# Who adds the last rows: two of four final adds move from VectorE to ScalarE and Pool

## The chip, the cores and the metric

The kernel runs on one core of one Trainium2 chip. The metric is the device time of one execution in microseconds (us), as the median of several executions. One profiled execution stands beside them; its span runs from the first to the last instruction of the core.

## The reference

One inference step of a two-layer encoder, for 256 rows of a new stream (the prompt) and 32 rows of a running one (the decode rows). Each layer is attention and then a feed-forward part; the second layer's is a mixture of 8 experts, of which every row uses two. Only the very end matters here: the weighted sum over the experts, added to the residual.

```python
def moe(h, router, wg, wu, wd):
    ...
    out = jnp.zeros_like(h)
    for e in range(N_EXPERTS):
        out = out + comb[..., e:e + 1].astype(h.dtype) * swiglu(h, wg[e], wu[e], wd[e])
    return out
...
        xp = xp + channel_mix(rms_norm(xp, ln_ffn[l]), l, *fw)      # (1, 256, 1024)
...
        xs = xs + channel_mix(rms_norm(xs, ln_ffn[l]), l, *fw)      # (1, 32, 1024)
```

`xp` and `xs` after the second layer are the outputs `y_prompt` and `y_sample`.

## The kernel before

Each engine has a program of its own, written out by hand in one order, and they meet at semaphores. The 288 rows are three tiles: two of 128 prompt rows and one of 32 decode rows. The residual of all three is `xres` (128 partitions x 3 tiles x 1024 columns) in SBUF; the decode rows are partitions 0 to 31 of tile 2. `ps` is the PSUM, eight banks of 512 float32 columns.

The experts run one after another. TensorE multiplies the gathered rows of one expert with weights that SP streams in. All experts but the last add their rows to a table in DRAM (`sum_rows`), by an indirect DMA of Pool. While the last expert runs, Pool loads that table back into `xres` (L893, L894; semaphore `sums_in`) and makes the 0/1 matrices `sel` (L898) that put each row of the last expert's result in its place.

The end of the program, after the last expert's products, works in two halves of 512 columns:

- ScalarE scales the result out of PSUM into `y_hi` (L1258 for half 0, L1264 and L1266 for the two parts of half 1; L1262 puts the last quarter of the columns in `y_out` first). VectorE takes the remainder of the split into `y_lo` (L1822, three times; semaphore `y_low`).
- TensorE multiplies `sel` with `y_hi` (L2448) and with `y_lo` (L2451), for three tiles each. Half 0 goes to the banks 0, 1 (prompt) and 4 (decode), half 1 to the banks 2, 3 and 5. When the second tile of a half is finished, and again when the third is, it raises `rows_full`.
- VectorE adds the banks to `xres` (L1829 both prompt tiles, L1831 the decode rows) and raises `rows_summed` after each.
- SP waits for those and issues four transfers to the outputs (L747 `y_p`, L750 `y_s`), 512 KB and 64 KB a half, then waits until all four have landed.

```python
banks = (2 * half, 2 * half + 1, 4 + half)
```

Of the kernel before, what the change touches and what calls it, by code (L numbers as in the profile page):

```python
# [22 lines left out]
ALU = mybir.AluOpType  # L23
ACT = mybir.ActivationFunctionType
# [5 lines left out]
SEQ, DEC = 256, 32  # L30
# [188 lines left out]
def build(nc, a, out, consts):  # L219
# [35 lines left out]
    with ExitStack() as ctx:  # L255
        def sb(name, shape, dt=F32):
            return ctx.enter_context(nc.sbuf_tensor(name, shape, dt))

        def sem(name):
            return ctx.enter_context(nc.semaphore(name))  # L260
# [8 lines left out]
        xres = sb("xres", [P, 3, D])  # L269
# [115 lines left out]
        y_out = carve("y_out", D)  # L385
# [21 lines left out]
        ps = ctx.enter_context(nc.psum_tensor("ps", [P, 8, 512], F32))  # L407
# [104 lines left out]
        sums_in = sem("sums_in")  # L512
# [3 lines left out]
        y_low = sem("y_low")  # L516
        rows_full = sem("rows_full")
        rows_summed = sem("rows_summed")
        result_out = sem("result_out")

        xs_rows = nc.dram_tensor("xs_rows", (SPARE, D), F32, kind="Internal").ap()
# [3 lines left out]
        def C(name, rows=P):  # L525
            at, w = CONST[name]
            return cst[0:rows, at:at + w]
# [14 lines left out]
        def pair(key, rows=P):  # L542

            *_, b, n = found(key)
            return ps[0:rows, b:b + n, :].rearrange("p a b -> p (a b)")
# [11 lines left out]
        def wide(b, rows=P):  # L557

            return ps[0:rows, b:b + 2, :].rearrange("p a b -> p (a b)")
# [6 lines left out]
        def wait_full(eng, key):  # L566
            filled, _, i, n, *_ = found(key)
            eng.wait_ge(filled[i], n)

        def wait_out(eng, key):  # L570
            _, emptied, i, n, *_ = found(key)
            eng.wait_ge(emptied[i], n)
# [75 lines left out]
        def _(sp):  # L648
# [36 lines left out]
            for key in plan:  # L685
# [8 lines left out]
                if key[0] == "wo":  # L694
                    _, _, c, typ = key
# [47 lines left out]

            for half in range(2):
                c0 = 512 * half
                sp.wait_ge(rows_summed, 2 * half + 1)
                sp.dma_start(out["y_p"][0].rearrange("(t p) d -> p t d", p=P)[:, :, c0:c0 + 512], xres[:, 0:2, c0:c0 + 512])\  # L747
                    .then_inc(result_out, 16)
                sp.wait_ge(rows_summed, 2 * half + 2)
                sp.dma_start(out["y_s"][0][:, c0:c0 + 512], xres[0:DEC, 2, c0:c0 + 512]).then_inc(result_out, 16)  # L750
            sp.wait_ge(result_out, 64)

# [1 line left out]
        def _(pool):  # L754
# [6 lines left out]
            for l in range(DEPTH):  # L761
                for n, name in enumerate(("b_qn_norm", "b_kn_norm")):
                    c = DEPTH * (n + 1) + l
# [132 lines left out]
            pool.wait_ge(row_split, 1)  # L896
            for t in range(3):
                pool.tensor_scalar(sel[0:SLOTS, t, :], C("iota", SLOTS), float(P * t), row_at[0:SLOTS, 0:1], ALU.add, ALU.is_equal).then_inc(sel_ready, 1)  # L898
            pool.wait_ge(stored, 16 * (DEPTH * 10))


        @block.scalar
        def _(act):
            A = nc.scalar.activation
# [45 lines left out]
            for l in range(DEPTH):  # L950
                for step in ACT_ORDER[l]:
# [20 lines left out]
                    elif kind == "zev":  # L972

                        t, c = which
# [243 lines left out]
            def expert(j, final):  # L1218

                A(warm[:, 0:1], warm[:, 0:1], ACT.Silu)  # L1220

                def silu(c):

                    w = WIDTH[c] // 2
                    act.wait_ge(unit_used, j * len(EXPERT) + (unit["gate", c, 3] + 1))
                    if c:
                        act.wait_ge(act_done, j * CHUNKS + c)
                    A(sgm[0:HALF, BANK:BANK + w], ps[HALF:P, 1, 0:w], ACT.Copy).then_inc(gate_part, 1)  # L1228
                    A(sgm[:, 0:w], ps[:, 0, 0:w], ACT.Silu)
                    act.wait_ge(gate_sum, j * CHUNKS + (c + 1))  # L1230
                    A(sgm[0:HALF, BANK:BANK + w], sgm[0:HALF, BANK:BANK + w], ACT.Silu).then_inc(silu_done, 1)

                def up_half(c):

                    w = WIDTH[c] // 2
                    act.wait_ge(unit_used, j * len(EXPERT) + (unit["up", c, 3] + 1))
                    if c:
                        act.wait_ge(am_ready, j * CHUNKS + c)
                    A(act_m[0:HALF, BANK:BANK + w], ps[HALF:P, 3, 0:w], ACT.Copy).then_inc(up_part, 1)  # L1239

                def output():

                    act.wait_ge(row_moved, j + 1)
                    act.wait_ge(unit_used, j * len(EXPERT) + len(EXPERT))
                    A(sgm[0:HALF, BANK:2 * BANK], ps[HALF:P, 7, :], ACT.Copy).then_inc(y_tail, 1)
                    for s_ in range(4):
                        g, h = s_ // 2, s_ % 2
                        A(y_out[GRAN * g:GRAN * g + GRAN, BANK * h:BANK * h + BANK], ps[GRAN * s_:GRAN * s_ + GRAN, 6, :], ACT.Copy)\
                            .then_inc(y_copied, 1)
                    act.wait_ge(y_copied, j * 4 + 4)  # L1250
                    act.wait_ge(y_sums, j + 1)
                    A(y_out[0:SLOTS, :], y_out[0:SLOTS, :], ACT.Copy, scale=slot_gate[0:SLOTS, 0:1]).then_inc(y_taken, 1)

                def last_output():

                    act.wait_ge(row_moved, j + 1)
                    act.wait_ge(y_half, 1)
                    A(y_hi[0:SLOTS, 0:512], ps[0:SLOTS, 6, :], ACT.Copy, scale=slot_gate[0:SLOTS, 0:1]).then_inc(y_high, 1)  # L1258
                    for g in range(MAIN):
                        if D_TAIL * (g + 1) > 512:  # L1260
                            act.wait_ge(y_half, 2)
                        ins = A(y_out[GRAN * g:GRAN * g + GRAN, D_LANE:D], wide(6)[SLOTS:P, D_TAIL * g:D_TAIL * g + D_TAIL], ACT.Copy)  # L1262
                    ins.then_inc(y_tail, 1)
                    A(y_hi[0:SLOTS, 512:D_LANE], ps[0:SLOTS, 7, 0:D_LANE - 512], ACT.Copy, scale=slot_gate[0:SLOTS, 0:1]).then_inc(y_high, 1)  # L1264
                    act.wait_ge(y_tail, j + 1)
                    A(y_hi[0:SLOTS, D_LANE:D], y_out[0:SLOTS, D_LANE:D], ACT.Copy, scale=slot_gate[0:SLOTS, 0:1]).then_inc(y_high, 1)  # L1266

                for c in range(CHUNKS):
                    silu(c)
                    up_half(c)  # L1270
                if final:
                    last_output()
                else:
                    output()

            last = act.snap(more * NE + (NE - 1))
            with act.Fori(0, last) as j:
                expert(j, False)
            expert(last, True)


        @block.vector
        def _(dve):
            V = nc.vector
# [128 lines left out]
            for l in range(DEPTH):  # L1413
                for step in DVE_ORDER[l]:
# [204 lines left out]
                    elif kind == "wd":  # L1619

                        t, c = which
# [203 lines left out]
            def result_rows(half):  # L1825

                c = slice(512 * half, 512 * half + 512)
                dve.wait_ge(rows_full, 2 * half + 1)
                V.tensor_tensor(xres[:, 0:2, c], xres[:, 0:2, c], ps[:, 2 * half:2 * half + 2, :], ALU.add).then_inc(rows_summed, 1)  # L1829
                dve.wait_ge(rows_full, 2 * half + 2)  # L1830
                V.tensor_tensor(xres[0:DEC, 2, c], xres[0:DEC, 2, c], ps[0:DEC, 4 + half, :], ALU.add).then_inc(rows_summed, 1)  # L1831

            result_low(1, ps[0:SLOTS, 6, :], slice(0, 512))
            result_low(2, ps[0:SLOTS, 7, 0:D_LANE - 512], slice(512, D_LANE))
            result_low(3, y_out[0:SLOTS, D_LANE:D], slice(D_LANE, D))
            dve.wait_ge(sums_in, 32)
            result_rows(0)
            result_rows(1)


# [679 lines left out]
```

## Time and profile before

| what | value |
|---|---|
| runs | 1217.24, 1217.74, 1217.84 us; median 1217.74 us |
| the profiled execution, its own time | 1219.62 us |
| its span | 1217.8 us |
| TensorE (matmul) busy | 1196.2 us, 98% of the span |
| VectorE busy | 552.8 us, 45% |
| ScalarE busy | 329.3 us, 27% |
| Pool busy | 79.0 us, 6% |
| DMA, mean over the span | 286 GB/s |

The profiled execution is one run with the profiler on: durations inside it are compared with each other, and its own time need not be that of the runs. Busy shares are means over a span with many stages, and say little of the last six microseconds. In rows of a timeline a number after "x" is how many instructions one row stands for; an instruction's duration can reach into that of the next on its engine.

### The profile page before, as it was taken

Reading aid. Unit: us, or ns where it says so; the run is one execution under the profiler, and the core shown is the slowest. Engines: PE = TensorE matmul, PEld = TensorE weight load, DVE = VectorE, ACT = ScalarE, POOL = GpSimd, SP = SyncE. Lnnn points to the kernel's source line nnn. Section 1 sums busy time; section 2 is a strip of 40 time slices with the busy share of each in tenths; the row PEclk is TensorE's granted clock in tenths of the full one; section 3 lists DMA queues with packets and bytes.
Section 4 is the critical chain, followed back from the end, with each engine's and each line's share of the span. In section 5 each row is a group of like instructions: output and inputs, shape, how many; then the busy total and the mean of one; then the engine's idle time right before and its main releaser. Section 6 shows DMA issues by size and latency. Waiting matters only on the chain.

```text
span 1217.8 us, 24127 instructions
## 1 busy us (share of the span) xinstructions
PE 1196.2 (98%) x10189; PEld 627.6 (52%) x10189; DVE 552.8 (45%) x1027; ACT 329.3 (27%) x602; POOL 79.0 (6%) x175
## 2 busy tenths in 40 slices
PE   8999999999999999999999999999999999999898
PEld 5466599999995466533333333333333333333255
DVE  1666644444414568533433434344264245334334
ACT  2557544333324565411210210200200201201101
POOL 4231000000001102000000000000000100100100
PEclk9999999999999999999999999999999999999999
DMA  9161195444250153699999999999999999999995
GB/s 302 31 165 61 42 304 173 150 163 154 88 173 31 24 117 107 242 410 399 410 388 411 402 395 413 398 400 414 399 402 414 399 399 415 389 411 414 393 410 233
DMA packets 113913, 348.51 MB, mean 286 GB/s; under 512 B 8401, under 2 KB 33841, under 8 KB 103617
## 3 DMA queue, kind: packets, MB, share of 16 engines
q1 hardware_dynamic: 108656, 335.55, 72.9%
q0 software_dynamic: 3648, 10.60, 3.1%
q10 hardware_dynamic: 1552, 1.56, 0.4%
q8 instruction: 41, 0.67, 0.2%
q14 instruction: 16, 0.12, 0.0%
HBM read 339.65 MB, written 8.04 MB: 286 GB/s over the span
## 4 chain that ended last, share of the span: by engine, by line
PE 90%; DMA 4%; DVE 3%; ACT 2%; SPq 0%; issue 0%; DVEq 0%; ACTq 0%
PE ps L2342 35%; PE ps L2349 17%; PE ps L2247 12%; PE ps L1991 8%; PE ps L2263 6%; DMA ring_more<-in_moe_w_gate 2%; DMA ring<-in_w_in 2%; PE ps L2064 1%; PE ps L2072 1%; PE ps L2328 1%; PE ps L2124 1%; PE ps L2139 1%; PE ps L2177 1%; PE ps L2187 1%; PE ps L2004 1%; PE ps L2333 1%
## 5 line engine op out<-in xcount | busy, mean ns | idle before, releaser
L2342 PE MATMUL ps<-ring,xg 128*32 128x512 f32 (+1 forms) x1792 | 203.9, 562 | 0.4 <-DVE xg L1723 0.4
L1774 DVE STREAM_TRANSPOSE am<-act_m 32x256 f32<-32x256 f32 (+1 forms) x288 | 172.5, 599 | 4.7
L2342 PE MATMUL ps<-ring_more,xg 128*32 128x512 f32 (+1 forms) x1280 | 144.6, 554 | 4.2 <-DMA ring_more<-in_moe_w_gate 4.2
L2342 PEld LDWEIGHTS ps<-ring,xg 128*32 128x32 f32 x1792 | 58.8, 110 | 119.7 <-issue 118.9
L1300 DVE TENSOR_TENSOR w_lo<-ring,w_hi 128x2048 fp32r<-128x2048 f32 (+1 forms) x34 | 75.8, 2230 | 96.1 <-ACT w_hi L914 96.1
L1991 PE MATMUL ps<-ring,hT 128*128 128x512 f32 x256 | 115.2, 596 | 0.1
L1759 DVE TENSOR_TENSOR act_m<-act_m,ps 64x512 f32<-64x512 f32 (+1 forms) x24 | 15.2, 635 | 213.3 <-ACT act_m L1239 213.3
L2349 PE MATMUL ps<-ring,xg 128*32 128x512 f32 (+1 forms) x896 | 110.0, 562 | 0.0
L2247 PE MATMUL ps<-hT_hi,w_hi 128*128 128x288 f32 x352 | 104.3, 296 | 0.5 <-DVE hT_lo L1642 0.5
L2247 PE MATMUL ps<-hT_lo,w_hi 128*128 128x288 f32 x352 | 103.8, 295 | 0.0
L2247 PE MATMUL ps<-hT_hi,w_lo 128*128 128x288 f32 x352 | 103.5, 294 | 0.0
L2342 PE MATMUL ps<-ring_more,am 128*32 128x512 f32 x784 | 95.7, 592 | 0.0
L1228 ACT ACTIVATE sgm<-ps 64x512 f32<-64x512 f32 (+1 forms) x24 | 13.4, 558 | 271.9 <-PE ps L2342 271.9
L914 ACT ACTIVATE w_hi<-ring 128x2048 fp32r<-128x2048 f32 (+1 forms) x34 | 63.3, 1863 | 82.4 <-PE ps L2247 44.1
L2342 PEld LDWEIGHTS ps<-ring_more,xg 128*32 128x32 f32 x1280 | 41.7, 111 | 84.5 <-issue 77.9
L1751 DVE TENSOR_TENSOR sgm<-sgm,ps 64x512 f32<-64x512 f32 (+1 forms) x24 | 15.2, 635 | 146.9 <-ACT sgm L1228 146.9
L2349 PE MATMUL ps<-ring_more,xg 128*32 128x512 f32 (+1 forms) x640 | 77.2, 553 | 0.0
L1991 PEld LDWEIGHTS ps<-ring,hT 128*128 128x128 f32 x256 | 46.8, 190 | 51.6 <-issue 51.4
L2247 PEld LDWEIGHTS ps<-hT_hi,w_hi 128*128 128x128 f32 x352 | 66.0, 187 | 0.9 <-DVE hT_lo L1642 0.9
L2247 PEld LDWEIGHTS ps<-hT_hi,w_lo 128*128 128x128 f32 x352 | 66.3, 188 | 0.0
L2247 PEld LDWEIGHTS ps<-hT_lo,w_hi 128*128 128x128 f32 x352 | 66.1, 188 | 0.0
L1239 ACT ACTIVATE act_m<-ps 64x512 f32<-64x512 f32 (+1 forms) x24 | 13.4, 558 | 182.4 <-PE ps L2342 182.4
(369 smaller groups left out, 1577.4 us busy)
## 6 DMA issues: line engine op xcount, KB each, us to landing
ring<-in_moe_w_up SPq DMA_DIRECT2D x48, 1024.0 KB, 18.6
ring_more<-in_moe_w_down SPq DMA_DIRECT2D x48, 1024.0 KB, 18.1
ring<-in_moe_w_gate SPq DMA_DIRECT2D x32, 1024.0 KB, 16.5
ring_more<-in_moe_w_gate SPq DMA_DIRECT2D x32, 1024.0 KB, 19.9
ring<-in_moe_w_down SPq DMA_DIRECT2D x32, 1024.0 KB, 16.2
ring_more<-in_moe_w_gate SPq DMA_DIRECT2D x32, 768.0 KB, 19.8
ring<-in_moe_w_up SPq DMA_DIRECT2D x32, 768.0 KB, 14.8
ring_more<-in_moe_w_up SPq DMA_DIRECT2D x16, 1024.0 KB, 17.4
```

The source lines that it names most:

```text
L914: A(hi[:, 0:size], src[:, 0:size], ACT.Copy).then_inc(hi_ready, 1)
L1228: A(sgm[0:HALF, BANK:BANK + w], ps[HALF:P, 1, 0:w], ACT.Copy).then_inc(gate_part, 1)
L1239: A(act_m[0:HALF, BANK:BANK + w], ps[HALF:P, 3, 0:w], ACT.Copy).then_inc(up_part, 1)
L1300: V.tensor_tensor(lo[:, 0:size], src[:, 0:size], hi[:, 0:size].bitcast(F32), ALU.subtract).then_inc(lo_ready, 1)
L1751: V.tensor_tensor(part, part, ps[0:HALF, 1, 0:w], ALU.add).then_inc(gate_sum, 1)
L1759: V.tensor_tensor(part, part, ps[0:HALF, 3, 0:w], ALU.add).then_inc(up_sum, 1)
L1774: ins = V.transpose(am[GRAN * q:GRAN * q + GRAN, c % 2, 0:nk, GRAN * g:GRAN * g + GRAN], src)
L1991: ins = mm_(pair(key), hT[:, k, TOFF[t]:TOFF[t] + P], slot(wk, 4, 512)[:, k % 4, :], start=(k == 0), stop=(k == KD - 1))
L2247: ins = mm_(pair(key)[:, 512 * f:512 * f + TOK], w[:, k, f * P:(f + 1) * P], x[:, k, :], start=(k == 0 and m == 0), stop=(k == KD - 1 and ...
L2263: ins = mm_(pair(("dn", i, d // 2))[:, 512 * (d % 2):512 * (d % 2) + TOK], w[:, k, d * P:(d + 1) * P], x[:, kk, :], start=(kk == 0 and m = ...
L2342: ins = mm_(ps[GRAN * s_:GRAN * s_ + GRAN, b, 0:half], x[:, GRAN * g:GRAN * g + GRAN], w[:, half * h:half * h + half], start=(n == 0), sto ...
L2349: ins = mm_(ps[r0:r0 + GRAN, b + 1, 0:half], x[:, GRAN * 2:SLOTS], w[:, half * h:half * h + half], start=(n < 2), stop=(n >= n_last - 1))
```

## The change

The decode rows of each half go another way. ScalarE, which has nothing left to do at that point, copies their PSUM bank into `y_out` in SBUF (new semaphore `decode_rows`). Pool, which can't read PSUM here, adds `y_out` to `xres` (new semaphore `decode_summed`). VectorE keeps the two prompt adds. `y_out` still holds the last quarter of the expert's columns for the third `y_lo` product, so ScalarE first waits for all three of these (`y_low` at 3). SP issues its four transfers in the same order, and waits for `decode_summed` ahead of each `y_s`.

```diff
@@ SP
-                sp.wait_ge(rows_summed, 2 * half + 1)
+                sp.wait_ge(rows_summed, half + 1)
                 sp.dma_start(out["y_p"][0]...
-                sp.wait_ge(rows_summed, 2 * half + 2)
+                sp.wait_ge(decode_summed, half + 1)
                 sp.dma_start(out["y_s"][0]...
@@ Pool, behind the three sel
+            pool.wait_ge(sums_in, 32)
+            for half in range(2):
+                c = slice(512 * half, 512 * half + 512)
+                pool.wait_ge(decode_rows, half + 1)
+                pool.tensor_tensor(xres[0:DEC, 2, c], xres[0:DEC, 2, c], y_out[0:DEC, c], ALU.add).then_inc(decode_summed, 1)
             pool.wait_ge(stored, 16 * (DEPTH * 10))
@@ ScalarE, behind the last expert
+            act.wait_ge(y_low, 3)
+            for half in range(2):
+                c = slice(512 * half, 512 * half + 512)
+                act.wait_ge(rows_full, 2 * half + 2)
+                A(y_out[0:DEC, c], ps[0:DEC, 4 + half, :], ACT.Copy).then_inc(decode_rows, 1)
@@ VectorE, result_rows(half)
                 V.tensor_tensor(xres[:, 0:2, c], xres[:, 0:2, c], ps[:, 2 * half:2 * half + 2, :], ALU.add).then_inc(rows_summed, 1)
-                dve.wait_ge(rows_full, 2 * half + 2)
-                V.tensor_tensor(xres[0:DEC, 2, c], xres[0:DEC, 2, c], ps[0:DEC, 4 + half, :], ALU.add).then_inc(rows_summed, 1)
```

How the instructions stand at the end of three engines' programs (the line numbers of the changed kernel are larger by 2 to 12). VectorE, from the three `y_lo` products to its last instruction, before:

```order
L1822 SCALAR_TENSOR_TENSOR y_lo<-ps,slot_gate,y_hi 96x512 [waits y_high]
L1822 SCALAR_TENSOR_TENSOR y_lo<-ps,slot_gate,y_hi 96x256 [waits y_high]
L1822 SCALAR_TENSOR_TENSOR y_lo<-y_out,slot_gate,y_hi 96x256 [waits y_high]
L1829 TENSOR_TENSOR xres<-xres,ps 128x2x512 [waits rows_full,sums_in]
L1831 TENSOR_TENSOR xres<-xres,ps 32x512 [waits rows_full]
L1829 TENSOR_TENSOR xres<-xres,ps 128x2x512 [waits rows_full]
L1831 TENSOR_TENSOR xres<-xres,ps 32x512 [waits rows_full]
```

and of the change:

```order
L1834 SCALAR_TENSOR_TENSOR y_lo<-ps,slot_gate,y_hi 96x512 [waits y_high]
L1834 SCALAR_TENSOR_TENSOR y_lo<-ps,slot_gate,y_hi 96x256 [waits y_high]
L1834 SCALAR_TENSOR_TENSOR y_lo<-y_out,slot_gate,y_hi 96x256 [waits y_high]
L1841 TENSOR_TENSOR xres<-xres,ps 128x2x512 [waits rows_full,sums_in]
L1841 TENSOR_TENSOR xres<-xres,ps 128x2x512 [waits rows_full]
```

The two adds of 32x512 are gone, and the second prompt add follows the first. ScalarE, its end in the changed kernel (before, its program ended with the fifth of these rows):

```order
L1265 ACTIVATE y_hi<-ps,slot_gate 96x512 [waits y_half,row_moved]
L1269 ACTIVATE y_out<-ps 32x256 x2
L1269 ACTIVATE y_out<-ps 32x256 [waits y_half]
L1271 ACTIVATE y_hi<-ps,slot_gate 96x256
L1273 ACTIVATE y_hi<-y_out,slot_gate 96x256 [waits y_tail]
L1291 ACTIVATE y_out<-ps 32x512 [waits rows_full,y_low]
L1291 ACTIVATE y_out<-ps 32x512 [waits rows_full]
```

Two copies out of PSUM stand behind everything that ScalarE did before. Pool, its end in the changed kernel (before, the last wait stood right behind the three `sel`):

```order
L897 CAST row_at<-slot_row 96x1
L900 TENSOR_SCALAR sel<-cst,row_at 96x128 [waits row_split]
L900 TENSOR_SCALAR sel<-cst,row_at 96x128 x2
L905 TENSOR_TENSOR xres<-xres,y_out 32x512 [waits decode_rows,sums_in]
L905 TENSOR_TENSOR xres<-xres,y_out 32x512 [waits decode_rows]
L255 UNCONDITIONAL_BRANCH [waits stored]
```

Two adds from SBUF to SBUF stand ahead of Pool's last wait. The order of TensorE's instructions and of SP's is the same in both kernels.

## Rows read from the trace of the kernel before

**Rows 1.** The page, chain that ended last: shares of the span by engine.

```profile
PE 90%; DMA 4%; DVE 3%; ACT 2%; SPq 0%; issue 0%; DVEq 0%; ACTq 0%
```

**Rows 2.** Timeline, 1205 to 1218: start us, us, engine, line, operation.

```profile
1210.27 0.86 PE L2451 MATMUL ps<-y_lo,sel 96*128 96x512 f32 x3
...
1210.88 0.48 DVE L1822 SCALAR_TENSOR_TENSOR y_lo<-y_out,slot_gate,y_hi 96x256 fp32r<-96x256 f32 x1
...
1211.27 1.21 DVE L1829 TENSOR_TENSOR xres<-xres,ps 128x1024 f32<-128x1024 f32 x1
...
1211.69 0.86 PE L2451 MATMUL ps<-y_lo,sel 96*128 96x512 f32 x3
1212.40 0.67 DVE L1831 TENSOR_TENSOR xres<-xres,ps 32x512 f32<-32x512 f32 x1
1212.51 0.42 SPq L747 DMA_DIRECT2D out_y_p<-xres  x1
1213.00 1.20 DVE L1829 TENSOR_TENSOR xres<-xres,ps 128x1024 f32<-128x1024 f32 x1
1213.10 0.36 SPq L750 DMA_DIRECT2D out_y_s<-xres  x1
1214.13 0.67 DVE L1831 TENSOR_TENSOR xres<-xres,ps 32x512 f32<-32x512 f32 x1
1214.23 0.39 SPq L747 DMA_DIRECT2D out_y_p<-xres  x1
1214.83 0.34 SPq L750 DMA_DIRECT2D out_y_s<-xres  x1
```

**Rows 3.** The chain that ended last, 1209 to 1218, its last piece.

```profile
1214.20 0.60 DVE xres L1831
```

**Rows 4.** SP queue's waits, 1170 to 1218: total us, times, longest.

```profile
SPq L255 <- DMA out_y_s<-xres: 2.2, 1, 2.2
```

**Rows 5.** DMA issues, 1205 to 1218: count, KB each, us to landing.

```profile
out_y_p<-xres SPq DMA_DIRECT2D x2, 512.0 KB, 2.9
out_y_s<-xres SPq DMA_DIRECT2D x2, 64.0 KB, 2.5
```

**Rows 6.** Windows of 0.1 us; the last three columns: TensorE clock, DMA share, GB/s.

```profile
1213.40:1213.50 0.10, 0.00 (x0) 0.00 (x0) 0.10 (x1) 0.00 (x0) 0.00 (x0) 1.00 0.50 184
...
1215.00:1215.10 0.10, 0.00 (x0) 0.00 (x0) 0.00 (x0) 0.00 (x0) 0.00 (x0) 1.00 0.47 144
1215.10:1215.20 0.10, 0.00 (x0) 0.00 (x0) 0.00 (x0) 0.00 (x0) 0.00 (x0) 0.64 0.54 185
1216.80:1216.90 0.10, 0.00 (x0) 0.00 (x0) 0.00 (x0) 0.00 (x0) 0.00 (x0) 0.50 0.28 82
```

**Rows 7.** Groups by line and shape, ScalarE: busy us, mean ns, idle before.

```profile
L1248 ACT ACTIVATE y_out<-ps 32x512 f32<-32x512 f32 x28 | 16.5, 589 | 0.7
```

**Rows 8.** Groups by line and shape, Pool: busy us, mean ns, idle before.

```profile
L898 POOL TENSOR_SCALAR sel<-cst,row_at 96x128 fp32r<-96x128 f32 x3 | 2.2, 726 | 0.1
...
L818 POOL COPY qkb<-kr 128x256 f32<-128x256 f32 x4 | 1.6, 402 | 19.4 <-PE ps L2088 19.4
...
L786 POOL TENSOR_TENSOR rc_a_q_norm<-cst,gains 128x128 f32<-128x128 f32 x2 | 0.9, 456 | 0.2
...
L787 POOL TENSOR_TENSOR rs_b_qr_norm<-cst,gains 128x32 f32<-128x32 f32 x2 | 0.5, 244 | 0.0
```

**Rows 9.** Timelines of ScalarE and of Pool near 1036.

```profile
1035.29 1.15 ACT L1252 ACTIVATE y_out<-y_out,slot_gate 96x1024 f32<-96x1024 f32 x1
...
1036.52 0.18 POOL L856 TENSOR_TENSOR tick<-cst 128x1 f32<-128x1 f32 x1 [64.75 <-ACT y_out L1252]
```

**Rows 10.** Timelines of VectorE and Pool, near 445 and near 368.

```profile
444.98 0.81 DVE L1510 TENSOR_TENSOR z<-z,rsz 128x640 f32<-128x640 f32 x1
...
445.07 0.83 POOL L800 TENSOR_TENSOR rt<-rtk,rc_b_kr_norm 128x32 f32<-128x32 f32 x1
...
367.81 0.40 DVE L1378 TENSOR_TENSOR xres<-xres,ps 128x256 f32<-128x256 f32 x1
...
367.90 0.40 POOL L818 COPY qkb<-cache_kr 128x256 f32<-128x256 f32 x1 [249.10 <-PE ps L1883]
```

More of the change, by code:

```diff
@@ L518, in build @@
         rows_summed = sem("rows_summed")
+        decode_summed = sem("decode_summed")
+        decode_rows = sem("decode_rows")
         result_out = sem("result_out")
```

## The prediction

> **What bounds the kernel now.** Read the chain first. Over the whole span 90% of it is TensorE and 4% DMA [rows 1], so an edit that touches neither can only act where that chain is not TensorE: at the very end. The timeline of the last microseconds shows that place [rows 2]. TensorE's last product ends at 1211.69 + 0.86 = 1212.55. From 1211.27 VectorE adds four times without a pause: prompt half 0 from 1211.27, decode half 0 from 1212.40, prompt half 1 from 1213.00, decode half 1 from 1214.13 to 14.80 (I write 14.80 for 1214.80 from here on). SP issues each of the four output transfers within 0.10 us after the add that feeds it ends, at 12.51, 13.10, 14.23 and 14.83. The chain of this stretch is those adds, its last piece the decode add of half 1 [rows 3], and SP's last long wait, 2.2 us, is for the last y_s transfer [rows 4]. By issue and time to landing [rows 5] the prompt half 1 lands at 14.23 + 2.9 = 17.13 and the decode half 1 at 14.83 + 2.5 = 17.33. The span ends at 1217.8, so 0.47 us follow that landing, which I keep.
>
> The reader should see one more thing before counting any gain. The DMA engines begin to move output between 13.40 and 13.50, and between there and 16.90 their only idle time is around 15.0 to 15.2, where the busy share drops to 0.47 and 0.54 [rows 6]. That is (0.53 + 0.46) × 0.1 = 0.10 us. So the four adds look like the bound, but behind them 1.18 MB goes out through DMA engines that are nearly full already.
>
> **The change, part by part.** Tensor products, their order and all transfers stay as they are; the order of TensorE has 2083 rows before and after. Nothing ahead of 1211.27 is touched.
>
> *VectorE* loses two adds of 32x512. The next add begins at 13.00 after 12.40 and 0.60 is thus the price of one on the path. Prompt half 0 is unchanged and ends at 12.48. Prompt half 1 can begin at 12.40, where the decode add began, if its two banks are full; TensorE's half 1 runs to 12.55 and its last of three products fills the decode bank, so the second is done some 0.2 us before that. I take 12.40, ending at 13.61 instead of 14.20: the y_p transfer of half 1 could be issued 0.6 us earlier.
>
> *ScalarE* gains two copies of 32x512 from PSUM. The same shape and direction took 0.59 us, 28 times [rows 7]; the extremes of the neighbourhood (0.1 us either way) don't matter below. ScalarE has nothing queued behind them. The first waits for TensorE's half 0 (10.27 + 0.86 = 11.13) and for the third y_lo product of VectorE (10.88 + 0.48 = 11.36) [rows 2]. The second condition ends last: 11.36 + 0.03 of hand-over (as from the add at 14.80 to SP's 14.83) + 0.59 = 11.98. The second copy starts when TensorE ends: 12.55 + 0.03 + 0.59 = 13.17.
>
> *Pool* gains two adds of 32x512, both inputs in SBUF, and has no such row. The nearest are its adds or products of two SBUF inputs, 0.456 us for 128 elements a partition and 0.244 us for 32 [rows 8]. The slope is 0.212/96 = 2.21 ns, so 512 elements take 0.456 + 384 × 0.00221 = 1.30 us. Bounds: from below the copies of 256 elements at 0.40 us, doubled, 0.80; from above the three compares that make sel, 0.726 for 128, times four, 2.90 [rows 8]. I take 1.30, because those rows are the same kind of operation with the same number of inputs. The hand-over from ScalarE to Pool is 1036.52 − (1035.29 + 1.15) = 0.08 us [rows 9]. So: first add 12.06 to 13.36, second (its copy is ready at 13.17, Pool is not) 13.36 to 14.66. Behind Pool's wait stands only its last wait for stores that are long done.
>
> *SP* issues in the written order: y_p half 0, y_s half 0, y_p half 1, y_s half 1. This is the wait the change adds on the path: y_s half 0 now waits for Pool until 13.36 (13.07 before), and y_p half 1 stands behind it. y_s half 0 is issued at 13.39, takes 0.36, y_p half 1 goes at 13.75 (13.61 had no queue been there), y_s half 1 at 14.69.
>
> *The sum.* Let a be Pool's add. y_s half 1 lands at 12.06 + 2a + 0.03 + 2.5 = 14.59 + 2a. With a = 1.30 that is 17.19, 0.14 us earlier than 17.33. The transfers give the other limit: y_p half 1 issued at 13.75 begins to move about 0.94 later (12.51 to 13.45 for the first), at 14.69, before the first two are through; so the idle 0.10 us closes, and nothing else can. The last byte and the landing come 0.10 us earlier, 17.23. The later of the two decides: −0.10 us. Pool at 0.80 would change nothing, since the transfers decide then; if the second half moved as fast as the first (1.60 us for 13.45 to 15.05 against 1.75 for 15.15 to 16.90) it would be −0.25.
>
> The profiled execution took 1219.62 us for a span of 1217.8, so 1.82 lie outside it, and it stood 1.88 above the median of the three runs, 1217.74. I apply the difference to the median: **1217.64 us**. It is 0.01%; a measurement of this kernel tells about 0.2% (2.44 us) from no change, so the forecast is "no change that can be seen".
>
> **Does Pool run beside VectorE?** The trace has both answers [rows 10]. While VectorE multiplied two SBUF tensors (444.98 to 445.79), Pool's product of 32 elements took 0.83 us and ended 0.11 after VectorE did, against 0.244 undisturbed. While VectorE added PSUM to an SBUF tensor (367.81 for 0.40), Pool's copy took its normal 0.40. VectorE's last adds have one input in SBUF and one in PSUM, so the second pair is the nearer. The Trainium skill has this as a rule ("SBUF — State Buffer", Who interferes with whom): a VectorE instruction with two SBUF inputs locks out a GpSimd one that reads SBUF, one with a single SBUF input does not. The trace agrees, as far as one copy shows it. "Perfetto Trace Analysis" (Optimizing Scalar/DVE Operations), in the same skill, warns more broadly that moving work between these two engines might not help; by it the lock rival below would be the case.
>
> **Rivals.**
> - *Pool and VectorE exclude each other here after all.* For: the 0.83 us row; the undisturbed pair is a copy with one input, Pool's add has two. Pool would be ready at 12.06, but start at 12.48, when prompt half 0 ends, until 13.78. Prompt half 1 follows, 13.78 to 14.99, and Pool's second add, 14.99 to 16.29. y_s half 1 goes at 16.32 and lands at 18.82: +1.49, **1219.2 us**. That is 0.12%, still within 0.2%.
> - *Pool's add costs what sel costs* (the other side). Place: Pool's two adds in a row, ahead of SP's last issue. The kernel is slower at all from 14.59 + 2a = 17.33, a = 1.37, only 0.07 above my estimate; by over 0.2% from 14.59 + 2a = 17.33 + 2.44, a = 2.59. At 2.90 the last landing is 20.39: +3.06, **1220.8 us**. For: a Pool operation of this kernel did take 5.7 ns an element. Against: it has a scalar operand, two operations and another output type, and the two-input rows lie at 2.2.
> - *The whole of VectorE's saving passes through.* The last add on VectorE ends at 13.61 instead of 14.80; if the end followed it, −1.19, **1216.55 us**. Against: the transfers are busy to 16.90 and SP's order puts Pool's adds ahead of the prompt's half 1. For it the DMA engines would have to move faster than in any stretch of the trace.
>
> **How the numbers follow.** The forecast (the end is held by the transfers and Pool) has 0.74; its own range is 1217.0 to 1218.0, from the lowest of the three runs less 0.25 (1217.24 − 0.25) to the highest plus what a = 1.45 would add (1217.84 + 0.16). The lock has 0.10, sel's price 0.04, the whole saving 0.09, something not listed 0.03. The range 1216.8 to 1219.3 takes in the forecast and the lock, 0.84, and leaves out most of the whole saving and sel's price. Only sel's price and half of the unlisted make the kernel slower by over 0.2%: 0.05. None of the listed makes it faster by that much, 0.01. No visible change: 0.94.
>
> **What the profile after should show.** Prompt adds back to back on VectorE, the second ending near 13.6; ScalarE copies of 0.59 from about 11.4 and 12.6; Pool adds of 1.30 with no gap between them, the first beginning near 12.06; the second y_p issue near 13.75, right behind the y_s issue, and the last issue near 14.7; the DMA engines without the dip at 15.0 to 15.2, and a span near 1217.7. A Pool add near 2 us or more, or a prompt add of half 1 that starts after 13.3, makes the prediction wrong; so does any move of work ahead of 1211.

## The result

The changed kernel takes 1219.87 us (median of 22 runs), the kernel before 1217.83 us beside it: ratio 1.0016, 95% interval 1.0010 to 1.0022. That is 2.0 us slower, with an interval from 1.2 to 2.7, outside the predicted range of 1216.8 to 1219.3. The profiled execution has a span of 1219.3 us (before 1217.8).

The timeline of the last microseconds of the changed kernel answers to [rows 2]:

```profile
1210.59 0.48 DVE L1834 SCALAR_TENSOR_TENSOR y_lo<-y_out,slot_gate,y_hi 96x256 fp32r<-96x256 f32 x1
...
1210.99 2.34 DVE L1841 TENSOR_TENSOR xres<-xres,ps 128x1024 f32<-128x1024 f32 x2
1211.10 0.59 ACT L1291 ACTIVATE y_out<-ps 32x512 f32<-32x512 f32 x1 [0.55 <-DVE y_lo L1834]
1211.39 0.86 PE L2461 MATMUL ps<-y_lo,sel 96*128 96x512 f32 x3
1211.84 2.49 POOL L905 TENSOR_TENSOR xres<-xres,y_out 32x512 f32<-32x512 f32 x2 [75.75 <-ACT y_out L1291]
1212.22 0.41 SPq L749 DMA_DIRECT2D out_y_p<-xres  x1
1212.29 0.59 ACT L1291 ACTIVATE y_out<-ps 32x512 f32<-32x512 f32 x1 [0.61 <-PE ps L2461]
1213.13 0.36 SPq L752 DMA_DIRECT2D out_y_s<-xres  x1
1213.55 0.45 SPq L749 DMA_DIRECT2D out_y_p<-xres  x1
1214.36 0.33 SPq L752 DMA_DIRECT2D out_y_s<-xres  x1
```

TensorE's last product ends 0.30 us earlier in this execution (1211.39 + 0.86 = 1212.25, before 1212.55). Counted from there the last transfer is issued 2.11 us later, before 2.28, so 0.17 us earlier. The median times to landing are about as before ([rows 5]: 2.9 and 2.5):

```profile
out_y_p<-xres SPq DMA_DIRECT2D x2, 512.0 KB, 3.1
out_y_s<-xres SPq DMA_DIRECT2D x2, 64.0 KB, 2.5
```

So the outputs are out near 1214.36 + 2.5 = 1216.86, and the span still runs to 1219.3. SP's waits show a long stretch behind the landing:

```profile
SPq L255 <- DMA out_y_s<-xres: 2.3, 1, 2.3
SPq L255 <- PEq L255: 2.1, 1, 2.1
```

In the kernel before, the second of these waits was short:

```profile
SPq L255 <- PEq L255: 0.2, 1, 0.2
```

The 2.1 us are put down to TensorE's sequencer. L255 is no line of the kernel's work: it is where each engine's program ends in a drain, and all engines meet. What each did there stands under that line, with the duration in ns three times (one instruction) and the start. The changed kernel:

```profile
L255 PEldq DRAIN  x1: 1183/1183/1183, 1211.1 to 1211.1; - x1
...
L255 POOLq DRAIN  x1: 5999/5999/5999, 1213.1 to 1213.1; - x1
...
L255 SPq DRAIN  x1: 13/13/13, 1217.2 to 1217.2; - x1
L255 SPq EVENT_SEMAPHORE  x1: 17/17/17, 1219.3 to 1219.3; - x1
```

and the kernel before:

```profile
L255 POOLq DRAIN  x1: 11608/11608/11608, 1134.6 to 1134.6; - x1
...
L255 SPq DRAIN  x1: 13/13/13, 1217.6 to 1217.6; - x1
```

The reader should see two things. SP arrives at the meeting at 1217.2, and Pool's drain ends at 1213.1 + 6.0 = 1219.1, after which everything ends. And the kernel before had such a drain too, even longer, but Pool had finished its work at 1136.7, so it ended at 1146.2, 71 us before anyone waited. The view names TensorE, but TensorE's own drain had ended at 1211.1 + 1.2 = 1212.3.

SP's arrival also shows what the earlier issue was worth. By the starts in ns it stands 4.956 us behind TensorE's last product, before 5.004: of the 0.17 us at the issue 0.05 are left behind the landing.

### The profile page after: what moved, and what is told of

The parts are those of the page before. It is cut to its first block, busy times and chain, and to the rows that moved or that the text cites. A ratio compares the mean times of both kernels' runs of the same rounds, so it can differ in the third digit from the quotient of the medians.

```text
span 1219.3 us, 24131 instructions
## 1 busy us (share of the span) xinstructions
PE 1197.1 (98%) x10189; PEld 628.6 (52%) x10189; DVE 551.5 (45%) x1025; ACT 330.5 (27%) x604; POOL 81.5 (7%) x177
## 4 chain that ended last, share of the span: by engine, by line
PE 90%; DMA 4%; DVE 3%; ACT 2%; SPq 1%; issue 0%; POOL 0%; ACTq 0%; DVEq 0%; POOLq 0%
PE ps L2352 35%; PE ps L2359 17%; PE ps L2257 12%; PE ps L2001 8%; PE ps L2273 5%; DMA ring_more<-in_moe_w_gate 2%; DMA ring<-in_w_in 2%; PE ps L2074 1%; PE ps L2082 1%; PE ps L2338 1%; PE ps L2134 1%; PE ps L2149 1%; PE ps L2187 1%; PE ps L2197 1%; PE ps L2014 1%; PE ps L2343 1%
## 6 DMA issues: line engine op xcount, KB each, us to landing
ring_more<-in_moe_w_up SPq DMA_DIRECT2D x16, 1024.0 KB, 17.4
```

## The experiments

Since spans differ by up to 3 us between executions ahead of the end, I also give the **tail**: from the end of TensorE's last product to the end of the span. It is 5.24 us before and 7.06 us in the changed kernel. The first theory (D): Pool's closing drain ends 4.75 us behind Pool's last add and holds the meeting. The first rival (P): the adds and copies themselves are late. Each kernel was run 11 times beside the kernel before; a tail is that of one profiled execution.

**Leave out the drain.** The changed kernel, with

```diff
-        block = ctx.enter_context(nc.Block())
+        block = ctx.enter_context(nc.Block(no_gpsimd_drain=True))
```

> The changed kernel, its block built without Pool's closing drain; nothing else differs. Theory D (the time went to Pool's closing drain, which ends 4.75 us after Pool's last add and holds the final meeting of the engines): the engines meet when SP has seen the last transfer land, the span is 1.9 us shorter than that of the changed kernel (1219.3 - 1.9 = 1217.4) and the median 2 us lower, 0.1 to 0.4 us below the kernel before. Theory P (Pool's adds or ScalarE's copies cost the time on the path to the last transfer): as slow as the changed kernel, 1.0016 of before. Theory M (the end of Pool's program waits for something else, such as writes on their way): the wait moves to another instruction of Pool and the time stays.

Measured: 1.0003 (0.9994 to 1.0012), tail 5.26 us. SP's wait at the meeting is gone:

```profile
SPq L255 <- DMA out_y_s<-xres: 2.4, 1, 2.4
SPq L255 <- PEq L255: 0.2, 1, 0.2
```

The loss is the drain. The 0.1 to 0.4 us below the kernel before did not show, in the tail (0.02 above) or the median.

**A late operation of Pool that nobody needs.** The kernel before, with

```diff
+            pool.wait_ge(rows_summed, 4)
+            hold(1)                       # one 128x1 product into a scratch column
             pool.wait_ge(stored, 16 * (DEPTH * 10))
```

> The kernel before, and one tiny Pool operation (128x1, 0.19 us) that waits for VectorE's fourth add; no decode row goes through ScalarE or Pool. Theory D: the operation ends at 1214.8 + 0.1 + 0.2 = 1215.1, the drain 4.75 later at 1219.85, and the span is 1220.0, 2.2 us over before (1.0018), though no output depends on Pool. Theory P: no output waits for it, same as before.

Measured: 1.0017 (1.0008 to 1.0026), tail 7.53 us. Pool's timeline and the rows of L255:

```profile
1213.05 0.19 POOL L856 TENSOR_TENSOR tick<-cst 128x1 f32<-128x1 f32 x1 [76.86 <-DVE xres L1833]
```

```profile
L255 POOLq DRAIN  x1: 4804/4804/4804, 1213.2 to 1213.2; - x1
L255 SPq DRAIN  x1: 13/13/13, 1215.7 to 1215.7; - x1
```

The whole loss comes back without a decode row on ScalarE or Pool. P is out.

**The same operation earlier.** `y_half` at 1, instead of `rows_summed` at 4.

> The kernel before, and the same tiny Pool operation, waiting for TensorE's last products of half 0 (near 1206.9). Theory D: the drain ends 4.75 us after it, near 1211.9, hidden, and the time is that of before. Theory O (the drain ends a fixed time behind the last output transfer, 2.2 us after its landing in the changed kernel): the drain runs to about 1219.5 and the time is 2 us over before.

Measured: 1.0004 (0.9995 to 1.0013), tail 5.22 us. The drain ended at 1209.9, behind the operation and not behind the outputs:

```profile
1204.97 0.20 POOL L856 TENSOR_TENSOR tick<-cst 128x1 f32<-128x1 f32 x1 [68.93 <-PE ps L2434]
```

```profile
L255 POOLq DRAIN  x1: 4809/4809/4809, 1205.1 to 1205.1; - x1
```

**Half of the change.** Half 1's decode rows go back to VectorE, and SP waits for its add (`rows_summed` at 3) ahead of the last transfer:

```diff
-            for half in range(2):      # Pool and ScalarE
+            for half in range(1):
...
             result_rows(1)
+            dve.wait_ge(rows_full, 4)
+            V.tensor_tensor(xres[0:DEC, 2, 512:D], xres[0:DEC, 2, 512:D], ps[0:DEC, 5, :], ALU.add).then_inc(rows_summed, 1)
```

> The changed kernel with the decode rows of half 1 added by VectorE from PSUM, after both prompt adds; half 0 still goes through ScalarE and Pool. Theory D: Pool's last operation ends 1.25 us earlier than in the changed kernel (near 1213.1), the drain near 1217.85, so the span is near 1218.0: 1.25 us less than the changed kernel, 0.1 to 0.3 us over before. Theory O: the drain ends near 1219.1 as in the changed kernel. Theory P: half of the loss, 1.0 us over before.

Measured: 1.0002 (0.9993 to 1.0011), tail 5.83 us: 1.23 less than the changed kernel (D: 1.25). It is 0.59 over before, where D had 0.1 to 0.3: D compared spans, and TensorE had ended 0.30 us earlier in the changed kernel's. The drain again ends 4.75 behind the add, at 1216.0, and SP arrives at 1215.3:

```profile
1209.94 1.26 POOL L905 TENSOR_TENSOR xres<-xres,y_out 32x512 f32<-32x512 f32 x1 [73.88 <-ACT y_out L1291]
```

```profile
L255 POOLq DRAIN  x1: 5869/5869/5869, 1210.1 to 1210.1; - x1
L255 SPq DRAIN  x1: 13/13/13, 1215.3 to 1215.3; - x1
```

**What the 4.75 us count from.** A late wait with no operation behind it (the kernel before):

```diff
+            pool.wait_ge(rows_summed, 4)
             pool.wait_ge(stored, 16 * (DEPTH * 10))
```

> The kernel before, and at the end of Pool's program a wait for VectorE's fourth add, with no operation behind it. Theory L (a drain takes 4.7 us whenever it starts): it starts near 1214.9, ends near 1219.6, and the time is that of the late tiny operation, 1.0017. Theory W (the 4.7 us count from Pool's last operation, here long past): the drain is under 0.5 us and the time is that of before.

Measured: 1.0018 (1.0009 to 1.0027), tail 7.41 us. The drain takes 4.73 us with nothing running on Pool, so D as I had put it falls: they don't follow an operation, they belong to the drain itself.

```profile
L255 POOLq DRAIN  x1: 4729/4729/4729, 1214.0 to 1214.0; - x1
L255 SPq DRAIN  x1: 13/13/13, 1216.5 to 1216.5; - x1
```

A memset in place of the product,

```diff
+            pool.wait_ge(rows_summed, 4)
+            pool.memset(tick[:, 1:2], 0.0)
```

> The kernel before, and a 128x1 memset on Pool, which reads no tensor, waiting for VectorE's fourth add. If the 4.75 us follow any Pool operation: the drain ends 4.75 us behind it, the time is that of the late tiny product, 1.0017. If they follow only operations that read SBUF: the drain is short and the time is that of before.

gave 1.0016 (1.0007 to 1.0025), tail 7.44 us, the drain 4.73 us long: the kind of operation made no difference that these runs show.

**One drain more, early.** The changed kernel, behind the three `sel`:

```diff
+            pool.drain()
             pool.wait_ge(sums_in, 32)
```

> The changed kernel, and one more drain on Pool right behind the three compares, 75 us ahead of the adds. Theory C (the 4.7 us are a first-use cost, such as loading the code for a drain): the closing drain is under 1 us behind the last add and the time falls to that of before, 1.000. Theory D as it stands (every drain ends 4.75 us behind the operation before it): the closing drain is as long as in the changed kernel, 1.0016.

Measured: 0.9996 (0.9987 to 1.0005), tail 5.17 us, 0.07 under the kernel before. The closing drain starts beside the second add and ends with it (1210.20 + 2.48 = 1212.68; the drain at 1212.76):

```profile
1210.20 2.48 POOL L906 TENSOR_TENSOR xres<-xres,y_out 32x512 f32<-32x512 f32 x2 [74.41 <-ACT y_out L1292]
```

```profile
L255 POOLq DRAIN  x1: 1298/1298/1298, 1211.5 to 1211.5; - x1
```

So a drain pays for something once. Is it its first use, or what Pool left behind since the drain before? A row of every kernel here already speaks against the first use: Pool runs a drain at the very start, ahead of any transfer of its own, and it is short. In the kernel before:

```profile
L2507 POOLq DRAIN  x1: 169/169/169, 0.3 to 0.3; - x1
```

The next run asks it directly.

**One small Pool transfer behind the early drain.**

```diff
             pool.drain()
+            pool.dma_start(tick[:, :], consts[:, 0:3]).then_inc(small_in, 16)
+            pool.wait_ge(small_in, 16)
```

> The early-drain kernel, and behind that drain one small transfer issued by Pool (128x3 into a scratch tile nobody reads), landed long before the adds. Theory C (first use of a drain is what costs): the closing drain stays short, as in the early-drain kernel (0.07 us behind the last add), time of before. Theory S (a drain settles what Pool's own transfers left behind; the early drain had done it): the closing drain is again near 4.7 us behind the last add, time 1.0016.

Measured: 1.0004 (0.9995 to 1.0013), tail 5.15 us. The closing drain ends 0.17 us behind the last add, not 4.7 and not quite 0.07. S in that form falls. But 0.09 us for one transfer is near what 57 transfers, Pool's number in the changed kernel, would need each to make 4.7. That was the next theory (N), and it could be dosed.

**16 transfers of the kernel's own, and 24 small ones.** The changed kernel with `pool.drain()` ahead of the loop over the experts, behind 41 of the 57:

```diff
+            pool.drain()
             with pool.Fori(0, last) as j:
```

> The changed kernel with one more drain on Pool ahead of the loop over the experts: 41 of Pool's 57 transfers come before it, 16 (14 indirect, 2 plain) between it and the closing drain. Theory N (a drain spends a fixed time on each transfer that Pool issued since the drain before: (4.75 - 0.07) / 57 = 0.082 us): the closing drain ends 0.07 + 16 x 0.082 = 1.4 us behind the last add. Theory C (the first drain behind Pool's transfers pays once, later ones 0.07 to 0.17 whatever came between): under 0.2 us. Theory B (by bytes or rows, most of which are in these 16): 3 us or more. The time is that of before by N and C, since 1.4 us end ahead of the last landing.

and the early-drain kernel with

```diff
             pool.drain()
+            for n in range(24):
+                pool.dma_start(scratch[:, 4 * n:4 * n + 4], consts[:, 4 * n:4 * n + 4]).then_inc(small_in, 16)
+            pool.wait_ge(small_in, 16 * 24)
```

> The early-drain kernel with 24 small transfers issued by Pool behind that drain (128x4 each, into a scratch tile nobody reads), all landed before the adds. Theory N: the closing drain ends 0.07 + 24 x 0.082 = 2.0 us behind the last add. Theory C: under 0.2 us. Theory B: about what one small transfer left, 0.17 us, or a little more. The time is that of before in all three, since 2.0 us end about when the last landing does.

The added drain ahead of the loop, and the closing one, in the first kernel:

```profile
L878 POOLq DRAIN  x1: 3427/3427/3427, 521.3 to 521.3; - x1
```

```profile
L255 POOLq DRAIN  x1: 2620/2620/2620, 1213.0 to 1213.0; - x1
```

and the closing one in the second:

```profile
L255 POOLq DRAIN  x1: 3298/3298/3298, 1213.4 to 1213.4; - x1
```

All the later drains of Pool that began after Pool's transfers had landed, with the starts in ns where the rows round them to 0.1 us; "behind" is from the end of Pool's last operation, or from the drain's own start where nothing ran:

| kernel | Pool's transfers since its drain before | drain ends behind, us | 0.071 + 0.082 n |
|---|---|---|---|
| early drain; the attempt at the end of this section | 0 | 0.071; 0.073 | 0.07 |
| early drain, one transfer | 1 | 0.165 | 0.15 |
| drain before the loop, closing | 16 | 1.393 | 1.38 |
| early drain, 24 transfers | 24 | 2.039 | 2.04 |
| drain before the loop, the added one | 41 | 3.427 | 3.43 |
| late wait only; late memset | 57 | 4.729; 4.729 | 4.75 |
| changed kernel; late product; early product; half | 57 | 4.753; 4.737; 4.738; 4.755 | 4.75 |

N said 1.4 and 2.0 for the two middle rows before they ran; C (under 0.2) and B (3 us or more for the 16 large ones, little for the 24 small ones) are out.

The sum does not cover a drain that begins while Pool's transfers are still under way. Such are the closing drains of the kernel before and of the next kernel, and the added ones behind the three `sel`. That of the early-drain kernel:

```profile
L901 POOLq DRAIN  x1: 11968/11968/11968, 1133.6 to 1133.6; - x1
```

These took 11.6 to 12.0 us and ended 2.9 to 3.1 us behind the last packet of those transfers (in the kernel before the packet ended at 1143.3, the drain at 1146.2, 9.5 us behind Pool's last operation). Why 2.9 us, no run here shows. They cost nothing because Pool had nothing else to do then.

The drain ahead of the loop gives 0.9999 (0.9990 to 1.0008) and a tail of 5.17 us. The one with 24 transfers has its drain hidden too, tail 5.29 us, yet its median is 1.0010 (1.0001 to 1.0019), which no theory expected: that 1.2 us (0.1 to 2.3) is not at the end of the kernel. The profiles show where it is. From its 9000th product (1096.6) to its 9600th (1166.1) TensorE takes 69.56 us, in the early-drain kernel 68.22; this stretch holds the 24 small transfers (1146 to 1165). Of one part of it, first the early-drain kernel and then the one with 24 transfers (us, busy us of TensorE's products, its weight loads, VectorE, ScalarE, Pool; TensorE clock, DMA share, GB/s):

```profile
1154.00:1160.00 6.00, 6.00 (x64) 1.71 (x57) 0.57 (x1) 1.11 (x2) 0.00 (x0) 1.00 1.03 417
```

```profile
1154.00:1160.00 6.00, 5.62 (x56) 1.38 (x52) 0.68 (x1) 1.32 (x3) 5.44 (x11) 1.00 1.04 360
```

The DMA engines are full in both, but move less in the second, and TensorE pauses. That the small transfers hold up the weights is the nearest reading; no run tests it alone.

**ScalarE alone.** The changed kernel without Pool's part, VectorE adding the copied rows from SBUF:

```diff
-                pool.wait_ge(decode_rows, half + 1)       # and Pool's add
...
             result_rows(1)
+            for half in range(2):
+                c = slice(512 * half, 512 * half + 512)
+                dve.wait_ge(decode_rows, half + 1)
+                V.tensor_tensor(xres[0:DEC, 2, c], xres[0:DEC, 2, c], y_out[0:DEC, c], ALU.add).then_inc(decode_summed, 1)
```

> The changed kernel without Pool's part: ScalarE copies the decode rows out of PSUM, VectorE adds them from SBUF, each after both prompt adds; SP as in the changed kernel. Theory D: no late Pool operation, so SP's last landing ends the kernel; the decode adds end near 14.2 and 14.9, y_p half 1 is issued behind y_s half 0 near 14.6, the last landing near 17.5: same as before within 0.3 us. Theory P' (ScalarE's copies cost time): slower than before by up to 2 us.

Measured: 1.0001 (0.9992 to 1.0010). The tail is 5.69 us, 0.45 over before where I had said 0.3: y_s half 0 comes late, and y_p half 1 stands behind it at SP. The copies cost nothing that the median shows.

**An attempt at something better.** Early drain, and the prompt rows added and sent tile by tile. The part on VectorE is shown; TensorE raises `rows_full` after every tile, and SP issues one y_p transfer for each:

```diff
-                V.tensor_tensor(xres[:, 0:2, c], xres[:, 0:2, c], ps[:, 2 * half:2 * half + 2, :], ALU.add).then_inc(rows_summed, 1)
+                for t in range(2):
+                    dve.wait_ge(rows_full, 3 * half + t + 1)
+                    V.tensor_tensor(xres[:, t, c], xres[:, t, c], ps[:, 2 * half + t, :], ALU.add).then_inc(rows_summed, 1)
```

> The early-drain kernel, and VectorE adds the prompt rows of a half tile by tile (128x512, 0.68 us, 0.60 on the path, instead of 128x1024), with one y_p transfer for each. The first output is issued near 0.68 instead of 1.21 us after the first add starts, 0.53 us earlier; the adds end 0.1 us later than in the early-drain kernel. If the transfers bound the end, as the prediction had it: the stretch from TensorE's last product to the end of the span falls from 5.17 to about 4.7 us. If the last y_s issue and its 2.3 to 2.5 us do: 5.2 as before. Either way under 0.05% of the time, within what the comparison of the medians can tell from no change.

The tail is 4.75 us, 0.42 under the early-drain kernel and 0.49 under the kernel before. That is what was expected if the transfers bound the end (4.7), and not if the last issue does (5.2). The last transfer is issued 0.12 us later behind TensorE's end (2.22 against 2.10) and lands sooner behind its issue (SP's waits; 2.3 in the early-drain kernel):

```profile
SPq L255 <- DMA out_y_s<-xres: 1.7, 1, 1.7
SPq L255 <- PEq L255: 0.2, 1, 0.2
```

The median is 0.9996 (0.9987 to 1.0005): 0.5 us of 1218 can't be told from nothing in this way. It is no slower than the kernel before; that it is faster is seen in one profile's tail alone.

## Why the prediction was wrong

*What held, step by step.* The prompt adds run back to back and end 10.99 + 2.34 = 13.33, 1.08 us behind TensorE's last product (predicted 13.61 against 12.55, 1.06). ScalarE's copies take 0.59 each. Pool's adds take 1.25 and 1.27 us (1.30 estimated from 32 and 128 elements), without a gap, beginning 0.15 us behind the first copy's end instead of 0.08. The order at SP, with y_p half 1 right behind y_s half 0 (13.13 + 0.36, then 13.55), is the one described. The last issue stands 2.11 us behind TensorE's end (2.14 predicted).

*What failed* is the sentence on Pool: "Behind Pool's wait stands only its last wait for stores that are long done". Behind it stood also the closing drain. With it fell "0.47 us follow that landing, which I keep": that stretch is a meeting of all engines, and it ends 0.2 us behind whoever comes last (SP in the kernel before, Pool's drain in the changed one). The sum should have had a second candidate: Pool's last add at 14.33, plus 4.75, plus 0.2 = 19.3, against SP's 17.2 + 0.2 = 17.4. The difference, 1.9 us, agrees with the tail (1.82 longer) and lies within the interval of the medians (1.2 to 2.7).

The rival on the slower side named the right engine, and the wrong place and price: it put the loss in Pool's adds, ahead of SP's last issue, at 2.90 us an add. An add takes 1.25 us, the outputs were not late at all, and the loss lies behind the adds. That its 1220.8 us, like the lock's 1219.2, is nearer to the measured 1219.87 than the forecast is luck. Its break-even point, "a = 1.37", counted only the way through SP. The lock between Pool and VectorE did not appear: Pool's first add ran wholly beside VectorE's adds from PSUM in 1.27 us, as the second did partly in 1.25. The Trainium skill's rule ("SBUF — State Buffer", Who interferes with whom) says so for a VectorE instruction with one input in SBUF, and the trace agrees with it now for a Pool add of two inputs. The saving of VectorE's 1.2 us did not pass through, as said: 0.17 us are left at the last issue (predicted 0.14) and 0.05 at SP's arrival (predicted 0.10, held there by the transfers). With the closing drain out of the way the rest of the sum fits: the early-drain kernel is the changed one with a drain added, and its tail is 0.07 us below before, in one profile of each, with a median that can't be told from before. The dip of the DMA engines was to close; it only shrank: their share was 0.57 and 0.78 from 1214.8 to 1215.0 (before 0.47 and 0.54).

The forecast "no change that can be seen" was thus wrong too: 0.16% lies under the 0.2% I had set, but 22 runs of each kernel tell it from nothing (1.0010 to 1.0022).

## What to carry to other kernels

When work moves to an engine that had finished early, list what that engine does behind its last instruction, down to its end-of-program drain, and count from there to the meeting of the engines; it was free only because the engine was early. For Pool here that price is 0.07 us plus 0.08 us for each transfer it has issued since its drain before, once they have landed. A drain placed where Pool is idle buys it off, as the early-drain kernel shows. Fewer transfers issued by Pool should do so too, which was not run: by an estimate from these numbers, in the 2.85 us between Pool's last add and SP's arrival some 33 transfers would have stayed hidden (24 did). And where a view blames a wait at the end on an engine that had long been done, look at each engine's instructions on that line.

## What the runs showed of the hardware that was not expected

- A drain on Pool is not short where Pool has issued transfers, even though all had landed, 1.3 to 72 us before: 0.082 us each, alike for 128x4 loads and for indirect ones of 96 rows (16 and 24 of them lie on one line with 41 and 57). What it does in that time no run shows. It starts beside Pool's running operation but the time counts from that operation's end: 4.75 us behind the last add in the changed kernel, where it had begun 1.25 us earlier.
- Drains on SP took 13 ns at the same meeting, in every kernel here.
- A wait alone, with no operation, is enough to move Pool's drain to the end and cost the 2 us.
